# Moving the second half of a depthwise convolution to GpSimd, with its normalisation and product moved in the order of work

## The reference

```python
o_a = mla_mixer(...)                       # latent attention
o_b = conv_mixer(u2, b_glu, w_dw, b_dw, g_ln, b_ln, w_out, b_out)
o_c = nsa_mixer(...)                       # attention in three parts
g_a, g_b, g_c = split(sigmoid(gate_mix))
x = x + (g_a * o_a + g_b * o_b + g_c * o_c) @ w_out
x = x + square(relu(rms_norm(x, g_ffn) @ w_ff1)) @ w_ff2
```

```python
def conv_mixer(u2, b_glu, w_dw, b_dw, g_ln, b_ln, w_out, b_out):
    a, gate = split(u2 + b_glu, 2)
    u = a * sigmoid(gate)                  # gated input, 512 channels
    u = depthwise_conv(u, w_dw) + b_dw     # causal, 31 taps, one filter per channel
    u = silu(layer_norm(u, g_ln, b_ln))    # over the 512 channels
    return u @ w_out + b_out
```

## Time and profile before

| | |
|---|---|
| median of 3 runs | 3073.32 us |
| lowest, highest | 3069.81, 3073.4 us |
| profiled execution, own time | 3075.1 us |
| profiled execution, span | 3072.4 us |
| TensorE busy, share of the span | 2709.2 us, 88% |
| VectorE busy | 1305.2 us, 42% |
| ScalarE busy | 606.2 us, 20% |
| GpSimd busy | 485.8 us, 16% |
| mean granted TensorE clock | 0.932 |

### The profile page before, as it was taken

One profiled execution on the slowest core, in us unless ns is written; L12 is line 12 of the kernel. 1 busy time (PEld: TensorE's weight loads), 2 busy tenths in 40 slices (PEclk: granted clock), 3 DMA queues, 4 the chain that ended last, 5 costly groups with the idle time before them and its releaser, 6 DMA issues.

```text
span 3072.4 us, 55234 instructions
## 1 busy us (share of the span) xinstructions
PE 2709.2 (88%) x23298; PEld 1871.0 (61%) x23298; DVE 1305.2 (42%) x2811; ACT 606.2 (20%) x1310; POOL 485.8 (16%) x390
## 2 busy tenths in 40 slices
PE   8997899899977998999998688888898887787787
PEld 6786586377865853344587688877785633333333
DVE  2635300035352001045444444444412777777754
ACT  1241100012411000013322344333200111111111
POOL 0000000000000000000000433432000354444452
PEclk9898999998989999999999799989999999889898
DMA  4322243342222344422320000000233799999996
GB/s 184 137 83 83 110 163 139 123 154 110 108 86 110 143 159 160 182 82 110 137 79 31 1 3 2 2 2 3 117 141 123 299 421 421 421 421 422 421 421 289
DMA packets 55033, 507.09 MB, mean 165 GB/s; under 512 B 6080, under 2 KB 6080, under 8 KB 7488
## 3 DMA queue, kind: packets, MB, share of 16 engines
q0 software_dynamic: 37024, 269.12, 21.2%
q1 hardware_dynamic: 17824, 235.41, 20.0%
HBM read 503.46 MB, written 1.05 MB: 164 GB/s over the span
## 4 chain that ended last, share of the span: by engine, by line
PE 31%; DMA 11%; DVE 8%; PEld 4%; issue 2%; ACT 2%; DVEq 1%; POOL 1%; POOLq 0%; ACTq 0%; PEldq 0%; SPq 0%
PE psum L1460 28%; DMA mem<-weights,mem 11%; PEld psum L1460 4%; DVE mem L2659 3%; PE psum L1895 3%; DVE mem L2181 2%; DMA mem<-weights 1%; PE psum L1470 0%; POOL mem L2788 0%; DVE mem L2438 0%; ACT mem L2038 0%; DVEq L2457 0%; POOL mem L2710 0%; ACT mem L2166 0%; DVE mem L2587 0%
## 5 line engine op out<-in xcount | busy, mean ns | idle before, releaser
L1460 PE MATMUL psum<-mem 64*64 64x64 f32 (+6 forms) x17432 | 1060.2, 262 | 119.6 <-DMA mem<-weights 21.8
L521 PE MATMUL psum<-mem 128*128 128x256 f32 (+8 forms) x4228 | 1065.5, 420 | 25.6 <-DVE mem L1178 12.9
L1460 PEld LDWEIGHTS psum<-mem 64*64 64x64 f32 (+3 forms) x17432 | 818.2, 151 | 357.2 <-issue 236.2
L521 PEld LDWEIGHTS psum<-mem 128*128 128x128 f32 (+3 forms) x4228 | 768.1, 196 | 316.1 <-issue 225.4
L1895 PE MATMUL psum<-mem 128*128 128x512 f32 x1024 | 505.6, 653 | 135.3 <-ACT mem L2166 135.0
L1895 PEld LDWEIGHTS psum<-mem 128*128 128x128 f32 x1024 | 209.4, 209 | 430.8 <-issue 249.4
L2788 POOL DMA_INDIRECT mem<-weights,mem x256 | 308.2, 1204 | 593.1 <-PE psum L1895 296.1
L2710 POOL TENSOR_TENSOR mem<-mem 128x512 f32<-128x512 f32 (+1 forms) x112 | 160.3, 1449 | 1351.6 <-ACT mem L2015 1091.5
L2659 DVE CUSTOM_DVE_ANT_0 mem<-mem 128x1024 f32<-128x1024 f32 x256 | 307.9, 1225 | 145.7 <-DMA mem<-weights,mem 140.0
L2181 DVE TENSOR_TENSOR mem<-psum,mem 128x512 f32<-128x512 f32 (+1 forms) x224 | 150.9, 685 | 315.5 <-PE psum L1460 297.7
L2181 DVE TENSOR_TENSOR mem<-mem 128x4 f32<-128x4 f32 (+5 forms) x201 | 144.9, 729 | 105.8 <-ACTq L1951 82.7
(11 more groups left out here) (221 smaller groups left out, 1125.6 us busy)
## 6 DMA issues: line engine op xcount, KB each, us to landing
mem<-weights SPq DMA_DIRECT2D x102, 2048.0 KB, 7.3
mem<-weights SPq DMA_DIRECT2D x2, 2176.0 KB, 7.7
mem<-weights,mem POOLq DMA_INDIRECT x256, 22.2
mem<-weights SPq DMA_DIRECT2D x2, 1536.0 KB, 7.3
mem<-weights SPq DMA_DIRECT2D x3, 1024.0 KB, 9.2
mem<-weights SPq DMA_DIRECT2D x2, 1152.0 KB, 8.1
mem<-weights SPq DMA_DIRECT2D x2, 1120.0 KB, 4.9
mem<-x SPq DMA_DIRECT2D x1, 1024.0 KB, 5.8
```

Of the source, the lines that this page charges most:

```text
L521: ins = pe.matmul(out, lhsT, rhs, start=start, stop=stop, skip_group_check=skip)
L1460: ins = pe.matmul(out, lhsT, rhs, start=start, stop=stop, skip_group_check=skip)
```

## The change

The second half of the convolution (chunks 2 and 3) goes from VectorE to GpSimd. GpSimd waits for the vector constants and for the second step of a new signal, `latent_and_glu_ready`, which VectorE raises once for the scaled latents (TensorE waits for that step, as before for `latent_ready`) and once for the gated input. GpSimd uses two instructions for a tap: a product of `upad` with the broadcast tap into one half of `sg`, and a sum into `cacc`, each of 128 x 512 (two chunks at once). The product of tap k + 1 is issued ahead of the sum of tap k, with a drain after each sum. That is 31 products and 31 sums a layer. VectorE's `convolve((2, 3))` goes.

TensorE's order changes: the conv transposes come straight after `outputs(2)`, the Bg1 gates behind them, then the convT transposes, then branch C's output, then branch B's. ScalarE takes the root of the layer norm after the second of branch C's four gate groups instead of after the fourth. VectorE forms the SiLU's product after the first of branch C's four output banks instead of after all four and their sum.

```diff
--- before.py
+++ after.py
@@ -436,7 +436,7 @@
     hT_by_act, hT_by_dve = signal("hT_by_act", 2), signal("hT_by_dve", 2)
     glu_gate_ready = signal("glu_gate_ready")
     latent_root_ready = signal("latent_root_ready")
-    latent_ready = signal("latent_ready")
+    latent_and_glu_ready = signal("latent_and_glu_ready", 2)
     latentT_ready = signal("latentT_ready")
     qm_copied = signal("qm_copied")
     vm_ready = signal("vm_ready")
@@ -610,7 +610,7 @@
             token_major(act_ring, l, "cq", hT, km_view(item(l, "cq"), 384), 8, 0, 384)
             token_major(act_ring, l, "ckv", hT, km_view(item(l, "ckv"), 288), 8, 0, 288)
             channel_major(act_ring, l, "u_gate", hT, km_view(item(l, "u_gate"), 512), 8, 4)
-            pe.wait_ge(*latent_ready.at(l))
+            pe.wait_ge(*latent_and_glu_ready.at(l, 0))
             blocks = [cq[:, t, c * P:(c + 1) * P] for c in range(3) for t in range(TT)]
             blocks += [ckvr[:, t, c * P:(c + 1) * P] for c in range(2) for t in range(TT)]
             for i in range(0, 10, 4):
@@ -712,16 +712,16 @@
             probs_transposes(l, 2)
             chunk_pair(act_ring, l, "gate", hT, gate, 8, 2)
             outputs(l, 2, nsa_v(2))
-            channel_major(act_ring, l, "gate", hT, km_view(item(l, "Bg1"), 512), 8, 4)
             pe.wait_ge(*conv_ready.at(l))
             for t in range(TT):
                 transposes(dve_ring, l, "conv", [cacc[:, c, t * P:(t + 1) * P] for c in range(4)])
-            pe.wait_ge(*nsa_out_ready.at(l))
-            channel_major(dve_ring, l, "mix", oTn, km_view(item(l, "Co"), D), 4, 8)
+            channel_major(act_ring, l, "gate", hT, km_view(item(l, "Bg1"), 512), 8, 4)
             pe.wait_ge(*conv_normed.at(l))
             yn = cacc.rearrange("p c t -> p (c t)").rearrange("p (t n) -> p t n", t=TT)
             for c in range(0, 4, 2):
                 transposes(act_ring, l, "convT", [yn[:, t, (c + j) * P:(c + j + 1) * P] for j in range(2) for t in range(TT)])
+            pe.wait_ge(*nsa_out_ready.at(l))
+            channel_major(dve_ring, l, "mix", oTn, km_view(item(l, "Co"), D), 4, 8)
             pe.wait_ge(*conv_act_ready.at(l))
             channel_major(dve_ring, l, "mix", cvT, km_view(item(l, "Bo"), D), 4, 8)
             pe.wait_ge(*merged_ready.at(l))
@@ -897,11 +897,12 @@
             act.wait_ge(*merge_gate_used.at(l, 0))
             half_tanh(l, 2, 0)
             probs_copies(l, 2)
-            for c in (2, 4, 6):
+            half_tanh(l, 2, 2)
+            act.wait_ge(*ln_var_ready.at(l))
+            A(lsd, aggr[:, :, 1], ACT.Sqrt, bias=C["eps"]).then_inc(ln_root_ready.sem, 1)
+            for c in (4, 6):
                 half_tanh(l, 2, c)
             act.drain().then_inc(merge_gate_ready.sem, 1)
-            act.wait_ge(*ln_var_ready.at(l))
-            A(lsd, aggr[:, :, 1], ACT.Sqrt, bias=C["eps"]).then_inc(ln_root_ready.sem, 1)
             for c in range(0, 4, 2):
                 b = act_ring.take(act, l, "convT")
                 for j in range(2):
@@ -1051,7 +1052,7 @@
                 v.tensor_scalar(cq[:, t, :], cq[:, t, :], crs[:, t:t + 1], None, ALU.mult)
                 v.tensor_scalar(ckvr[:, t, 0:256], ckvr[:, t, 0:256], crs[:, 2 + t:3 + t], None, ALU.mult)
             v.tensor_copy(kf[:, :, :, 0:MROPE], bc(ckvr[:, :, 256:288], 2, MH))
-            v.drain().then_inc(latent_ready.sem, 1)
+            v.drain().then_inc(latent_and_glu_ready.sem, 1)
             v.wait_ge(*glu_gate_ready.at(l))
             for c in range(0, 4, 2):
                 b = dve_ring.take(v, l, "u_a")
@@ -1060,7 +1061,7 @@
                     last = v.scalar_tensor_tensor(upad[:, k, CONV_W - 1:], b[:, j * T:(j + 1) * T], V["b_glu"][:, k:k + 1],
                                                   sg[:, k, :], ALU.add, ALU.mult)
                 last.then_inc(dve_ring.free, 1)
-            v.drain()
+            v.drain().then_inc(latent_and_glu_ready.sem, 1)
             convolve((0, 1))
             for half in range(2):
                 for t in range(TT):
@@ -1152,8 +1153,6 @@
             add_outputs(l, 2)
             v.sem_inc(nsa_out_ready.sem, 1)
 
-            convolve((2, 3))
-            v.drain().then_inc(conv_ready.sem, 1)
             yn = cacc.rearrange("p c t -> p (c t)").rearrange("p (t n) -> p t n", t=TT)
             b2 = [dve_ring.take(v, l, "conv") for _ in range(TT)]
             for t in range(TT):
@@ -1169,13 +1168,14 @@
                 v.tensor_scalar(yn[:, t, :], b2[t], aggr[:, t, 0:1], lrs[:, t:t + 1], ALU.subtract, ALU.mult).then_inc(dve_ring.free, 1)
             v.drain().then_inc(conv_normed.sem, 1)
             v.wait_ge(*merge_gate_ready.at(l, 1))
-            for c in range(0, 8, 2):
+            gated(l, 1, 0)
+            v.wait_ge(*conv_silu_parts.at(l))
+            v.tensor_tensor(cvT, cvT, sg, ALU.mult).then_inc(conv_act_ready.sem, 1)
+            for c in (2, 4, 6):
                 gated(l, 1, c)
             v.drain()
             v.tensor_tensor(mg, mg, gsig[1], ALU.add)
             v.drain().then_inc(merge_gate_used.sem, 1)
-            v.wait_ge(*conv_silu_parts.at(l))
-            v.tensor_tensor(cvT, cvT, sg, ALU.mult).then_inc(conv_act_ready.sem, 1)
             v.wait_ge(*merge_gate_ready.at(l, 2))
             v.tensor_scalar(gsig[0], gsig[0], 1.0, None, ALU.add)
             v.drain()
@@ -1214,6 +1214,22 @@
             if l:
                 pool.wait_ge(*layer_done.at(l - 1))
             pool.dma_start(vec, V1[l]).then_inc(vec_landed, 16)
+            pool.wait_ge(vec_landed, l * 16 + 16)
+            pool.wait_ge(*latent_and_glu_ready.at(l, 1))
+            taps = V["w_dw"].rearrange("p (c k) -> p c k", c=4)
+
+            def tapped(k):
+                pool.tensor_tensor(sg[:, 2 * (k % 2):2 * (k % 2) + 2, :], upad[:, 2:4, k:k + T], bc(taps[:, 2:4, k], 2, T), ALU.mult)
+
+            tapped(0)
+            pool.drain()
+            for k in range(CONV_W):
+                if k + 1 < CONV_W:
+                    tapped(k + 1)
+                so_far = cacc[:, 2:4, :] if k else bc(V["b_dw"][:, 2:4], 2, T)
+                pool.tensor_tensor(cacc[:, 2:4, :], sg[:, 2 * (k % 2):2 * (k % 2) + 2, :], so_far, ALU.add)
+                pool.drain()
+            pool.sem_inc(conv_ready.sem, 1)
 
     first_block.close()
```

## The result

The changed kernel takes 3121.85 us (median of 4 runs, 3115.34 to 3124.01) against 3073.19 us for the kernel before beside it: ratio 1.015, interval 1.0138 to 1.0163. It is slower by 48.7 us, where 3117, slower by 44, was forecast.

A forecast was written before the change was run, and what follows sets the result against it. TensorE, busy 88% of the span, was taken as the bound. Per layer 49 - 1.1 + 2.2 - 27.7 = +22.4, rounded 22; two layers +44 gave 3117 us against the median, 8-in-10 range 3044 to 3160.

The forecast's parts named there:

- The delay: VectorE's first convolution half, sharing SBUF with GpSimd, ends at 143.8 us instead of 94.8: 49 us late per layer.
- turns: VectorE and GpSimd alternate strictly by instruction when both read SBUF, each finishing 0.90 to 1.08 us after the other.
- The tap of 2.6 us: One convolution tap: GpSimd product 0.90, sum 1.06, two VectorE scalar_tensor_tensor at 0.32 us; 30 taps take 78 us.
- The open point of the prediction: No row showed scalar_tensor_tensor against GpSimd; the rival that it takes no turns gave 3042 us, chance 0.12.
- the signs named for being right: L998 at 1.2 to 1.4 us, GpSimd's tensor_tensor likewise, TensorE idle some 48 us per layer, both old rests gone.
- the whole-instruction rival: In the convolution each engine holds for its whole single duration: 3.26 us per tap, 69 us late, 3157 us; chance 0.12.
- The slack of 1.06 us: At the second head norm, ScalarE waits 1.06 us on TensorE before copying the last kvn1 bank, giving VectorE that slack.
- The rest of about 48: TensorE rests about 48 us per layer before the transposes that wait for ScalarE's copy of the last kvn1 bank.
- The restart: After TensorE's long rest, work resumes at low clock, costing about 2.2 us per layer.
- The gain: Rests before conv transposes and branch B's output go, with their low clock: 16.92 + 6.45 + 4.3 = 27.7 us per layer.
- 22.4: Net loss per layer: 49 - 1.1 + 2.2 - 27.7 = +22.4 us, rounded to 22.

The follow-up runs named there:

- e3: The changed kernel with each GpSimd instruction cut into two of 128 x 256: 3069.41 us, ratio 0.9979 to the kernel before.
- e4: The changed kernel with GpSimd's products and sums replaced by memsets of the same tiles, chunks 2 and 3 left out: 3028.0 us, one run.
- e5: The changed kernel with GpSimd's products and sums replaced by one-operand copies, chunks 2 and 3 left out: 3062.07 us, one run.
- e7: The changed kernel with the convolution's second half back on VectorE at its old place, nothing on GpSimd: 3093.04 us, ratio 1.0054.
- e2: The changed kernel's order without GpSimd; VectorE runs chunks 2 and 3 in its own idle gaps: 3022.2 us, ratio 0.9828.
- e6: The kernel before with only the convolution's second half moved to GpSimd, order as it was: 3139.14 us, ratio 1.021.
- e1: The changed kernel with GpSimd starting only after the last full-width head norm: 3023.26 us, ratio 0.9823 to the kernel before.
- e1b: The changed kernel with GpSimd starting still later, after the compressed keys' norm: 3032.33 us, ratio 0.9856 to the kernel before.

## Why the prediction was right

**The delay.** Forecast: 49 us, from turns read in the second block of the kernel before. The root of the second head norm is at 160.15 us instead of 112.26: 47.9. The tap of 2.6 us measured 2.59; its parts were forecast as 0.90 + 1.06 + 2 x 0.32 and came as 0.90 + 1.13 + 0.28 + 0.27. The open point of the prediction, whether scalar_tensor_tensor takes turns like the scan and the tensor_tensor of the earlier trace rows, is settled: it does. e3 shows that the turn is one instruction (805 ns for halves), and e4 and e5 that for this form it needs GpSimd to read. One of the signs named for being right came only in part: of GpSimd's instructions, expected at 1.2 to 1.4 us, the sum takes 1.43 us and the product 1.05. The rule of the Trainium skill, "SBUF — State Buffer", section "Who interferes with whom", agrees here in what contends with a VectorE instruction of two SBUF operands: reads of GpSimd, not its writes (482 ns in e4). That the holder keeps the port for its whole instruction (for two operands the page says so in its section "SBUF: two separate sides") doesn't carry over to the rows as a sum of single durations: the product follows VectorE's end by 0.90 us where alone it shows 1.04, the sum by 1.13 where alone it shows 1.28. So the whole-instruction rival fell; its tap of 3.26 us would have given 3157.

**The path.** The slack of 1.06 us held: the root is 47.9 us late and the transposes start 46.7 late. The rest of about 48 (47.58 and 48.43) and its releaser were right. The restart in layer 0 cost 4.50 - 2.37 = 2.1 us (2.2 forecast). **The gain**: 83.58 - 55.53 = 28.05 us in layer 0 (27.7 forecast); e7 shows from the other side that it hangs on the sum being ready, and e2 that GpSimd isn't needed for it. Layer 0 sums to 46.7 + 2.1 - 28.05 = 20.8 us, which is what the start of `out` shows (346.78 to 367.55). The forecast was 22.4: the delay was 1.1 us shorter and the gain 0.35 larger.

**What was off.** At the first long matmul of the second block the changed kernel is 45.2 us behind (1223.40 to 1268.62), where the forecast was 44. The other 3.6 us of the two spans' difference lie in the second block, which is the same code: in the eleven profiles of this study it takes between 1845.0 (e6) and 1853.6 us (e4), 1849.0 in the kernel before and 1852.6 after, with no visible relation to the edit. Layer 1 cost 24.4 us instead of 20.8: 1.7 in `out`, 1.6 in the matmuls from the second gate pair to the scores (46.96 for 45.31 in layer 0), 0.9 in the longer rest, less 0.6 in the transposes behind it (3.94 for 4.50). The first two are low-clock stretches of a length that I hadn't counted and can't derive from these rows. So layer 0 came 1.6 us under the forecast of 22.4 and layer 1 2.0 over it; that the two together hit 44 within 1.2 us is in part luck, while the terms themselves, 49, 2.2 and 27.7, each held to about 1 us in layer 0.

## What to carry to other kernels

Work given to GpSimd while VectorE has two-operand SBUF work isn't free even where GpSimd itself has all the time in the world: count VectorE's instructions in that stretch, multiply by what one turn adds, and look whether what stands behind them has that much slack. Here a turn adds about 0.8 us beside GpSimd instructions of 1.04 and 1.28 us and 0.3 us beside halves of 0.60 to 0.71 us, which is some 0.35 us less than the GpSimd instruction's length alone: with the full lengths, 60 instructions would have come to 70 us instead of the 48 measured. Start the slow engine where the fast one is idle or reads PSUM, or leave it out: here VectorE's own gaps (e2) gave as much as GpSimd at its best. And a reordering and the offload that it relies on are to be priced together, since here either alone was slower than neither (3139 and 3093 us).

## What the runs showed of the hardware

The loss in a turn is one-sided. In e1, where GpSimd works alone for a while, a tap takes 2.42 us:

```profile
144.13 1.04 POOL L1222 TENSOR_TENSOR mem<-mem 128x512 f32<-128x512 f32 x1
145.13 1.28 POOL L1230 TENSOR_TENSOR mem<-mem 128x512 f32<-128x512 f32 x1
146.55 1.04 POOL L1222 TENSOR_TENSOR mem<-mem 128x512 f32<-128x512 f32 x1
```

With two VectorE instructions let in it takes 2.59: GpSimd lost 0.17 us a tap, 7%, while VectorE went from 0.476 to 1.30 us an instruction. VectorE's two turns take 0.55 us of the tap. Most of it is made up: product and sum end 0.90 and 1.13 us behind VectorE's end instead of being 1.04 and 1.28 long, together 0.29 less, and 0.10 us lay between instructions before (2.42 less 1.04 and 1.28). GpSimd's product even shows the same 1.04 us in both and its sum 1.44 for 1.28, so its own rows hardly give the contention away; it is VectorE's that have to be read.

The clock's low stretches are not tied to a rest alone. The `out` stage follows a wait of 2.31 to 2.34 us in every kernel here, and took 27.70 us in both layers of the kernel before but 29.40 in layer 1 of the changed one. There the granted clock was 0.70 in 994.4 to 1000 us and 1.00 from 1000 on. In e1b a rest as long (2.36 us) left the clock at 1.00. What sets off the one and not the other stays open.
